# Moving ScalarE's rounding of a weight tile from the tile's first block to its second

## The reference, cut to what matters

```
def deltanet_mixer(h, w_in, conv_w, a_log, dt_bias, o_norm, w_out):
    qkv, z, a, b = jnp.split(h @ w_in, [3 * W, 4 * W, 4 * W + DN_HEADS], axis=-1)
    qkv = jax.nn.silu(causal_dwconv(qkv, conv_w)).astype(jnp.float32)
    q, k, v = jnp.split(qkv, 3, axis=-1)
    q, k, v = l2norm(q.reshape(shp)), l2norm(k.reshape(shp)), v.reshape(shp)
    beta = jax.nn.sigmoid(b.astype(jnp.float32))
    g = -jnp.exp(a_log) * jax.nn.softplus(a + dt_bias)
    o = gated_delta_rule_chunked(q, k, v, g, beta)      # triangular solves of 64 x 64
    o = rmsnorm(o, o_norm) * jax.nn.silu(z.reshape(shp).astype(jnp.float32))
    return o.reshape(B, S, W).astype(h.dtype) @ w_out

def gla(u, w_in, gate_w1, gate_w2, gate_b, norm_gain, w_out):
    q, k, v, r = jnp.split(u @ w_in, [kd, 2 * kd, 2 * kd + vd], axis=-1)
    def log_gate(d):
        logits = (u @ gate_w1[d]) @ gate_w2[d] + gate_b[d]
        return split_heads(jax.nn.log_sigmoid(logits) / GLA_GATE_NORMALIZER, GLA_HEADS)
    o = bidirectional_scan(q, k, v, log_gate(0), log_gate(1))
    o = merge_heads(rmsnorm_2(o, norm_gain)) * jax.nn.silu(r)
    return o @ w_out
```

## Time and profile before

| | value |
|---|---|
| median of three runs | 2660.6 us |
| the profiled execution's own time | 2660.5 us |
| its span | 2658.7 us |
| mean granted TensorE clock | 0.996 of full |
| PE busy | 2606.3 us, 98% |
| DVE busy | 1817.0 us, 68% |
| ACT busy | 1406.8 us, 53% |

### The profile page before, as it was taken

One profiled execution on the slowest core, in us unless ns is written; L12 is line 12 of the kernel. 1 busy time (PEld: TensorE's weight loads), 2 busy tenths in 40 slices (PEclk: granted clock), 3 DMA queues, 4 the chain that ended last, 5 costly groups with the idle time before them and its releaser, 6 DMA issues. The chain is left out here.

```text
span 2658.7 us, 49223 instructions
## 1 busy us (share of the span) xinstructions
PE 2606.3 (98%) x21088; PEld 2524.1 (95%) x21088; DVE 1817.0 (68%) x2374; ACT 1406.8 (53%) x1934; POOL 0.2 (0%) x4
## 2 busy tenths in 40 slices
PE   9999999999999999999999999989999999999998
PEld 9999999999998999999899999889988999989998
DVE  7668766666668756676756866978565785756774
ACT  6546655454467365545456476354464545446543
POOL 0000000000000000000000000000000000000000
PEclk9999999999999999999999999999999999999999
DMA  7554545555544244555544555135543555544553
GB/s 269 180 193 162 176 151 192 197 191 191 196 153 123 88 159 145 199 192 180 188 140 159 191 195 178 48 128 194 194 150 108 185 192 192 178 155 156 177 194 131
DMA packets 129865, 450.12 MB, mean 169 GB/s; under 512 B 20208, under 2 KB 21104, under 8 KB 129520
## 3 DMA queue, kind: packets, MB, share of 16 engines
q1 hardware_dynamic: 129504, 446.83, 50.3%
q10 hardware_dynamic: 144, 0.14, 0.0%
HBM read 445.48 MB, written 1.44 MB: 168 GB/s over the span
## 5 line engine op out<-in xcount | busy, mean ns | idle before, releaser
L274 PE MATMUL B<-R,WH 128*128 128x256 f32 x10432 | 2023.2, 279 | 13.8 <-DVE R L1230 6.3
L274 PEld LDWEIGHTS B<-R,WH 128*128 128x128 f32 x10432 | 1655.2, 188 | 26.0 <-issue 9.8
L1015 DVE TENSOR_TENSOR WL<-SL,WH 128x1024 fp32r<-128x1024 f32 x835 | 1006.1, 1222 | 606.8 <-ACT WH L2095 605.1
L274 PE MATMUL B<-R,WL 128*128 128x256 f32 x4480 | 1240.1, 277 | 0.0
L2095 ACT ACTIVATE WH<-SL 128x1024 fp32r<-128x1024 f32 x835 | 862.5, 1053 | 453.5 <-PE B L274 437.7
L274 PEld LDWEIGHTS B<-R,WL 128*128 128x128 f32 x4480 | 844.7, 189 | 0.0
L274 PE MATMUL B<-RB,WH 128*128 128x256 f32 x1984 | 547.8, 276 | 0.2 <-DVE WL L1015 0.2
L274 PE MATMUL B<-RB,WL 128*128 128x256 f32 x1728 | 476.9, 276 | 0.0
L274 PEld LDWEIGHTS B<-RB,WH 128*128 128x128 f32 x1984 | 372.4, 188 | 0.5 <-DVE WL L1015 0.4
L274 PEld LDWEIGHTS B<-RB,WL 128*128 128x128 f32 x1728 | 324.4, 188 | 0.0
L274 PE MATMUL B<-WH,R 128*128 128x512 f32 x480 | 157.0, 398 | 0.0
(11 more groups left out here) (293 smaller groups left out, 1565.7 us busy)
## 6 DMA issues: line engine op xcount, KB each, us to landing
SL<-in_w SPq DMA_DIRECT2D x835, 512.0 KB, 3.3
CP<-in_cp SPq DMA_DIRECT2D x5, 768.0 KB, 4.9
PG<-in_mem SPq DMA_DIRECT2D x1, 1024.0 KB, 6.2
PK<-in_pk SPq DMA_DIRECT2D x1, 594.5 KB, 9.2
XG<-in_xT SPq DMA_DIRECT2D x1, 512.0 KB, 7.4
out<-XG SPq DMA_DIRECT2D x1, 512.0 KB, 2.6
SL<-in_w SPq DMA_DIRECT2D x1, 384.0 KB, 3.4
XG<-in_xT SPq DMA_DIRECT2D x1, 256.0 KB, 5.8
```

Source lines behind the costliest of these rows:

```text
L274: return p.matmul(o, left, right, start=first, stop=final, skip_group_check=True)
L1015: v.tensor_tensor(WL[t % NRAW][:, :], SL[t % NRAW][:, :], WH[t % NSPL][:, :].bitcast(F32), ALU.subtract).then_inc(s_lo, 1)
```

## The change

One condition in ScalarE's `walk`. Where `behind` is 0 nothing changes. Where it is 2, `hi` is issued at the block with remainder 1 in stages of width 1 and with remainder 2 in those of width 2: one step later either way. What it waits for is the same, and so is the tile. VectorE's `lo` stays: in stages of width 1 one step behind the new place, in those of width 2 at the same step. TensorE, VectorE and SyncE run the same lists as before.

```
@@ -2103,7 +2103,7 @@
                 st = ST[name]
                 for x, (j, k) in enumerate(st.order):
                     b = st.block + x * st.width
-                    if b and b % 4 == 0 and x >= skip and x not in ahead(name):
+                    if b and b % 4 == min(behind(name), st.width) and x >= skip and x not in ahead(name):
                         hi(b // 4 + 4)
                     yield j, k
```

## The result

Six runs of the changed kernel gave 2669.01 to 2670.64 us, median 2669.43; the kernel before, beside them, 2660.31 us. The ratio is 1.0034, 95% interval 1.0024 to 1.0044: slower by 9.1 us. Predicted were 2668.9 us, range 2662.0 to 2673.5.

The account below looks back on a forecast made before the run. TensorE, busy 2606.3 of 2658.7 us, bounds the kernel, so the change acts only through its waits. 6.75 us of waits with 1.7 of clock make 8.4, added to 2660.5: 2668.9 us, range 2662 to 2673.5.

Parts of the forecast that it names:

- x = 16 to 29: Delta rule: roundings now behind the scaling delay the spread, so TensorE starts a small product late; +1.2 us.
- x = 32 to 61: Delta rule: TensorE's wait of 1.86 us for the square becomes 2.8, late once, not twice; +1.25 us.
- x = 64 to 95: Delta rule: the scaling of x = 64 comes earlier, shortening the wait of 2.18 us for a normalisation; -0.2 us.
- x = 112 to 126: Delta rule: late roundings hold VectorE's `lo`, so the values of line 1540 reach TensorE late; +2.1 us.
- Gated linear attention: In g.v0 a late rounding holds `lo` and the sum, +2.85 us; at the stage's end spreads go first, -0.45 us.
- The clock: Half-clock losses behind TensorE's waits: two longer waits lose 0.85 and 1.7 us, a shortened one saves 0.85; +1.7 us.
- nothing else moves: Outside the delta rule and the gated linear attention nothing was to move.
- half of the waits: Rival: TensorE was not ready at two places or VectorE has hidden room; 3.5 us, 2664 us; chance 0.14.
- waits without clock: Rival: the waits come but the clock does not follow; 6.75 less 0 to 1.7, some 2666 us; chance 0.22.
- not slower: Rival: copies TensorE needs go ahead of roundings and nothing comes later; -2.5 us, 2658 us; chance 0.08.

Follow-up runs that it names:

- undo_16: Changed kernel with the delta rule's roundings of x = 16, 20 and 24 put back to the first block: 2668.47 us.
- undo_48: Changed kernel with the delta rule's roundings of x = 48 and 56 put back to the first block: 2669.40 us (eight of nine executions).
- undo_48a: Changed kernel with only the delta rule's rounding of x = 48 put back, that of x = 56 still late: 2670.16 us.
- undo_112: Changed kernel with the delta rule's roundings of x = 112 and 120 put back to the first block: 2666.73 us.
- undo_gv: Changed kernel with one rounding of 33 put back, that of step 4 in g.v0: 2665.83 us, ratio to before 1.0018.
- sum_first: Changed kernel with VectorE's first sum of line 1967 moved from step 5 to step 4 of g.v0, ahead of the subtraction: 2665.95 us, ratio to before 1.0017.
- gla_only: Kernel before with roundings late only in the gated linear attention: 2664.59 us, ratio 1.0014.
- changed again: The changed kernel measured once more, nothing altered: 2670.55 us, ratio to before 1.0035.
- gr_only: Kernel before with late roundings only in g.r, at 5 places: 2659.51 us, ratio 0.9994.

## Why the prediction was right

The time lies 0.5 us above the forecast, and the mechanism held: the waits came where the order of the lists puts them. That the sum fits so well is in part chance, for the clock and three smaller amounts were not as forecast. TensorE's lateness against before can be read at any product that both timelines show. It was 0.46 us at 760 us already, ahead of the first moved rounding. Then:

- x = 16 to 29, predicted +1.2: 782.32 became 784.18, that is 1.4 more; of it 1.08 are the two waits. One of the two, for the square at x = 27, I had not seen: the half microsecond of x = 16 reached TensorE there first. undo_16 removed both. The amount held, its split did not.
- x = 32 to 61, predicted +1.25: 818.97 became 822.15, 1.32 more. undo_48 and undo_48a show the two places sharing one delay.
- x = 64 to 95, predicted -0.2: 845.17 became 848.15, -0.20.
- x = 112 to 126, predicted +2.1: 913.37 became 918.38, +2.03. undo_112 puts it on these two roundings.
- Gated linear attention, predicted +2.85 and -0.45: the wait is 2.78, and of 0.73 all went. undo_gv and sum_first put it on one rounding and one subtraction.
- The clock, the step that was wrong as put, predicted +1.7 as 0.85 behind line 2445, 1.7 behind line 1967 and half of 1.7 saved behind line 1481. In the first profile the parts were 0, +1.7 and 0, and 1.7 more came behind the wait of 2.00 us for line 2701 at 2435 us, which the change had not made any longer. In the lateness the two losses behind lines 1967 and 2701 are 1.6 us each, 3.2 together, where 1.7 were predicted. The step as put (a wait longer than 2.18 costs clock, a shorter one may not) was wrong, see below, and that it held behind line 1967 proves nothing, as it failed behind the equally long wait for line 2445.
- Not foreseen: at 918 us TensorE was 5.01 us late, at 1973 us only 3.60 (1969.72 to 1973.32). Of this, 0.59 us went at 972 us, where the wait of 0.43 us for `lo` is gone: the change did that, and "nothing else moves" was wrong there. Another 0.73 us went in the retention, between 1746.84 (4.38 late) and 1771.90 (3.65 late), and is the clock's: its mean was 0.74 from 1742.46 to 1752 us in the kernel before, 2.5 us lost, and 0.82 from 1746.84 to 1756 us in the changed kernel, 1.6 us lost. The wait for line 1880 ahead of it, 1.45 us before and 0.36 now, gave nothing back. Its product starts 7.72 or 7.73 us after the one for line 1871 in all thirteen profiles, so it takes up what the clock leaves: none is left in gla_only and undo_48, 3.12 us in sum_first.
- Added up, the waits as placed by the prediction brought 6.6 us of lateness (predicted 6.75). To these come 0.46 from before the first moved rounding, -0.59 at 972 us, -0.73 in the retention, and 3.2 of clock, 8.9 in all; read at 2490 us it is 8.78.

The prediction's rival "half of the waits" adds 1.25 + 1 + 1.5 to 3.5 us; it is 3.75, which changes nothing here.

The rival "waits without clock" fits neither profile of the changed kernel; "half of the waits" is out since all came; and what "not slower" says, a copy that TensorE needs goes ahead of a rounding, held at two places, in g.r and in the cross attention. By what the Trainium skill (TensorE: Matmul & The Clock Gate, HAM oscillation) says of the idle gaps that let the clock fall, none of the waits of 1.86 to 2.82 us would cost clock; each loss shown above behind such a wait contradicts it.

## What to carry to other kernels

Work that others need late is best put where its engine waits anyway; moved from ahead of a wait to behind it, it adds its whole length to what comes next, and frees nothing (x = 48). Where a copy that TensorE needs gets ahead of it, the same move helps, here twice by less than 1 us. Before moving a producer, look at where its consumer stands on the next engine: a consumer that nobody needs yet still holds back all behind it, here 2.8 us for one rounding of 33, and moving the consumer cures it as well as moving the producer back. Two delays on one chain count once when the first reaches the second, and add up when the engine between them has no gap.

## What the runs showed of the hardware

Thirteen profiles, those of before and after and of the eleven runs above, give the span as a sum: the waits of PE, plus the clock losses up to 2640 us, plus 2606.6 to 2608.9 us. Seven of them:

| | waits | lost clock | span | rest |
|---|---|---|---|---|
| before | 42.2 | 8.5 | 2658.7 | 2608.0 |
| changed | 46.7 | 11.9 | 2667.5 | 2608.9 |
| changed again | 46.9 | 11.9 | 2667.2 | 2608.4 |
| undo_112 | 44.8 | 8.5 | 2662.0 | 2608.7 |
| undo_48a | 45.5 | 17.0 | 2669.9 | 2607.4 |
| gla_only | 42.6 | 11.9 | 2662.8 | 2608.3 |
| gr_only | 40.1 | 8.7 | 2656.5 | 2607.7 |

The waits that the change touches repeat to 0.05 us from run to run where no low clock stands just ahead of them; in the retention the wait for line 1880 runs from 0 to 3.12 us. The losses come in steps of 1.7 us and are drawn anew: behind waits of 2.8 us (lines 2445 and 1967) the clock fell to its half level in 11 of 14 cases, behind waits near 2.0 us (2.0 to 2.2 for line 1481, and twice 2.0 for line 2701) in 15 of 38, behind the 1.87 us of line 1540 in 3 of 8, behind the 1.86 us of line 2445 in 3 of 5. One more loss, of 1.7 or 3.4 us at 766 to 774 us, stands in 8 of the 13 with no wait right before it: the last is one of 0.97 us that ended at 760 us, and the low clock follows 32 small products, 3.64 us with TensorE busy (line 274, 128x16). So neither 1.86 us is safe, as I had taken it from one profile, nor does 2.8 always cost. Single runs of one kernel spread by 2 to 7 us (the kernel before: 2658.7 to 2665.3), most likely because of it, though only profiled executions show where clock was lost. One profile can't give the price of a wait in clock.
